# Routed experts fed by slot from DRAM, and a two and four step split of the wide experts

## The reference, cut to what matters

```python
top_val, top_idx = lax.top_k(xf @ router_w, 2)
gates = softmax(top_val)
# for each expert e, on the rows xb of the tokens that chose it:
y = (silu(xb @ w_gate[e]) * (xb @ w_up[e])) @ w_down[e]   # 1024 -> 2816 -> 1024
out[token] += gate * y
```

## Time and profile before

| | us |
|---|---|
| time before, median of 3 runs | 1365.17 (1364.94 to 1366.44) |
| the profiled execution | 1365.75 |
| its span | 1363.9 |
| PE busy | 1295.7 |
| DVE, ACT, POOL busy | 674.4, 555.1, 154.5 |

### The profile page before, as it was taken

The page is one execution under the profiler, slowest core; times in us unless marked ns, Lnnn a source line. Parts: engine busy times, 40 slices in busy tenths (PEclk is TensorE's granted clock), DMA queues, the critical chain, the costliest instruction groups (busy, mean ns, idle before and its releaser), DMA issues.

```text
span 1363.9 us, 25579 instructions
## 1 busy us (share of the span) xinstructions
PE 1295.7 (95%) x10975; PEld 1027.5 (75%) x10975; DVE 674.4 (49%) x894; ACT 555.1 (41%) x843; POOL 154.5 (11%) x201
## 2 busy tenths in 40 slices
PE   7999999999999999999999999799999999979994
PEld 7978988788888987988755777487555577747762
DVE  5766555766666565654510763265101076326512
ACT  5466444533346456644311651254000065225401
POOL 6300000000000800000122011203020201220200
PEclk9999999999999999999999999999999999999998
DMA  9307533455554413652799989998999999999895
GB/s 380 129 1 295 218 136 123 155 185 185 185 202 153 152 35 127 262 198 96 294 418 421 421 343 368 420 420 350 394 421 420 421 420 417 368 420 420 342 412 241
DMA packets 55150, 387.48 MB, mean 284 GB/s; under 512 B 6368, under 2 KB 6752, under 8 KB 9216
## 3 DMA queue, kind: packets, MB, share of 16 engines
q1 hardware_dynamic: 54112, 384.07, 70.8%
q10 hardware_dynamic: 432, 1.08, 0.2%
q0 software_dynamic: 496, 0.74, 0.2%
HBM read 383.77 MB, written 2.10 MB: 283 GB/s over the span
## 4 chain that ended last, share of the span: by engine, by line
PE 82%; DMA 8%; DVE 4%; ACT 3%; issue 1%; SPq 0%; ACTq 0%; DVEq 0%
PE banks L2268 21%; PE banks L1988 14%; PE banks L1989 14%; PE banks L1990 14%; DMA added<-in_pieces_dram 8%; PE banks L2192 6%; PE banks L2194 3%; PE banks L2227 3%; PE banks L2243 2%; PE banks L2139 1%; PE banks L2354 1%; PE banks L2167 1%; PE banks L2002 1%; PE banks L2012 1%; DMA raw<-in_pieces_dram 1%
## 5 line engine op out<-in xcount | busy, mean ns | idle before, releaser
L1455 DVE TENSOR_TENSOR w_low<-raw,w_high 128x2048 fp32r<-128x2048 f32 x93 | 214.5, 2308 | 138.1 <-ACT w_high L992 138.0
L992 ACT ACTIVATE w_high<-raw 128x2048 fp32r<-128x2048 f32 x93 | 178.2, 1918 | 105.4 <-PE banks L2194 65.5
L2268 PE MATMUL banks<-added,token_rows 128*32 128x128 f32 (+2 forms) x3088 | 154.5, 299 | 12.0 <-DMA added<-in_pieces_dram 8.9
L2268 PEld LDWEIGHTS banks<-added,token_rows 128*32 128x32 f32 (+1 forms) x3088 | 116.7, 118 | 49.4 <-issue 18.3
L1988 PE MATMUL banks<-rows,w_high 128*128 128x256 f32 x480 | 136.8, 285 | 3.1 <-DVE rows L1456 2.4
L1989 PE MATMUL banks<-rows,w_high 128*128 128x256 f32 x480 | 135.8, 283 | 0.0
L1990 PE MATMUL banks<-rows,w_low 128*128 128x256 f32 x480 | 135.8, 283 | 0.0
L2192 PE MATMUL banks<-rows,w_high 128*128 128x512 f32 x352 | 124.5, 398 | 1.3 <-DVE rows L1456 1.3
L1455 DVE TENSOR_TENSOR added_low<-added,piece_high 128x1024 fp32r<-128x1024 f32 x80 | 95.7, 1223 | 42.5 <-ACT piece_high L992 25.7
L1450 DVE TENSOR_SCALAR turned<-banks 128x128 f32<-128x128 f32 (+2 forms) x36 | 12.3, 342 | 188.0 <-PE banks L2354 188.0
L2194 PE MATMUL banks<-rows,w_low 128*128 128x256 f32 x352 | 98.8, 281 | 0.0
(11 more groups left out here) (259 smaller groups left out, 2315.5 us busy)
## 6 DMA issues: line engine op xcount, KB each, us to landing
raw<-in_pieces_dram SPq DMA_DIRECT2D x195, 1024.0 KB, 9.2
added<-in_pieces_dram SPq DMA_DIRECT2D x162, 1024.0 KB, 18.3
phase<-in_mem_dram SPq DMA_DIRECT2D x2, 1024.0 KB, 6.5
early<-in_constants_dram SPq DMA_DIRECT2D x1, 1088.0 KB, 13.7
h_res<-in_x_dram SPq DMA_DIRECT2D x2, 512.0 KB, 4.2
phase<-in_mix_norm_post_dram SPq DMA_DIRECT2D x2, 512.0 KB, 4.1
phase<-in_xa_norm_post_dram SPq DMA_DIRECT2D x2, 512.0 KB, 6.3
kept<-h_res SPq DMA_DIRECT2D x2, 512.0 KB, 10.2
```

The lines of the kernel that those rows point to most:

```text
L992: return act.activation(out_, in_, ACT.Copy, scale=scale)
L1455: return dve.tensor_tensor(out_, in_, plain(high), ALU.subtract)
L2268: return pe.matmul(dst, stay, move, start=start, stop=stop, skip_group_check=True)
```

## The change

Rows no longer come from a matmul with `place` (but for the first unit's). In the first layer POOL writes zeros to a new DRAM tensor `by_slot` of 8 x 256 rows. After routing, DVE works out for each token and each of its two choices the row number 256 * expert + rank, and POOL scatters the normed rows there, in four indirect DMAs of 128 rows. For each unit from the second on, POOL loads the first rows of its expert into a new tile `slot_rows` (128 + 32 rows for class 3, 64 for class 1, 32 for class 0), and PE turns them by transposes (`turn_rows`), in three turns for class 3 and in one otherwise. In the first unit these turns stand at its fourth and fifth step. `xn_high` and `xn_low` move into two slots of the ring that are filled later, and the space gives the ring an eleventh new slot, 17 in all. The wide experts are cut into steps (0, 2) and (2, 6) in place of (0, 3) and (3, 6).

```diff
-ADDED = 2 * SPLIT + 4
+ADDED = 2 * SPLIT + 5
-UNITS = ((1, 0, 6), (0, 0, 3), (3, 0, 6), (0, 3, 6), (2, 0, 6), (6, 0, 6), (5, 0, 3), (4, 0, 6), (5, 3, 6), (7, 0, 6))
+UNITS = ((1, 0, 6), (0, 0, 2), (3, 0, 6), (0, 2, 6), (2, 0, 6), (6, 0, 6), (5, 0, 2), (4, 0, 6), (5, 2, 6), (7, 0, 6))
...
-ROWS_AT = {WIDE_STEPS: {(1, "up"): 0, (2, "up"): 1, (3, "up"): 2, (4, "up"): 3, (5, "up"): "spread"},
-           WIDE_STEPS // 2: {(0, "up"): 0, (1, "up"): 1, (1, "out"): 2, (2, "up"): 3, (2, "mid"): "spread"}}
+ROW_TURNS = [ROW_PAIRS if u == 0 else 3 if STRAIGHT[u] == 3 else 1 for u in range(COUNT_UNITS)]
+ROW_LOADS = [0 if u == 0 else 2 if STRAIGHT[u] == 3 else 1 for u in range(COUNT_UNITS)]
+ROWS_AT = {(WIDE_STEPS, 3): {(1, "up"): 0, (2, "up"): 1, (3, "up"): 2, (5, "up"): "spread"},
+           (WIDE_STEPS, 1): {(2, "up"): 0, (5, "up"): "spread"},
+           "first": {(3, "up"): 0, (4, "up"): 1, (4, "out"): 2, (5, "up"): "spread"},
+           (2, 1): {(0, "up"): 0, (1, "mid"): "spread"},
+           (4, 1): {(1, "up"): 0, (3, "mid"): "spread"}}
...
+def row_turn(u, i):
+    if STRAIGHT[u] < 3:
+        return 0, MOST[STRAIGHT[u]], 0, KT
+    return (0, P, i * KT // 2, (i + 1) * KT // 2) if i < 2 else (1, QUARTER, 0, KT)
...
-        xn_low = sb("xn_low", [P, TT, D], F32R)
-        xn_high = sb("xn_high", [P, TT, D], F32R)
+        xn_high, xn_low = (added_low[:, i, :].rearrange("p (t d) -> p t d", t=TT) for i in (2 * SPLIT - 2, 2 * SPLIT - 1))
+        slot_rows = sb("slot_rows", [P, 2, D])
...
-        ring = [RAW + (2 * SPLIT + i) % ADDED for i in range(ADDED)] + [(more_from + i) % RAW for i in range(RAW)]
+        ring = [RAW + i for i in (6, 7, 8, 9, 0, 1, 2, 3, 10, 4, 5)] + [(more_from + i) % RAW for i in range(RAW)]
...
+                if c == more_from + 8:
+                    sp.wait_ge(h_kept, TT * 16)
+                    sp.wait_ge(row_high, TT)
+                if c == more_from + 9:
+                    sp.wait_ge(gathered, ROW_PAIRS)
...
+            chain(pool.memset(zeros[:, :], 0.0))
...
+                if layer == 0:
+                    for b in range(EXPERTS * TT):
+                        pool.dma_start(by_slot[b * P:(b + 1) * P, :], zeros[:, :]).then_inc(zeroed, 16)
...
-            def places(e):
...
+            def load_rows(u):
+                n = UNITS[u][0]
+                for block in range(ROW_LOADS[u]):
+                    count = (MOST[STRAIGHT[u]] if STRAIGHT[u] < 3 else P) if block == 0 else QUARTER
+                    first_row = n * SEQ + block * P
+                    pool.dma_start(slot_rows[0:count, block, :], by_slot[first_row:first_row + count, :]).then_inc(rows_in, 16)
+            pool.wait_ge(zeroed, EXPERTS * TT * 16)
+            pool.wait_ge(row_gained, TT)
+            pool.wait_ge(indexed, 1)
+            for choice in range(2):
                 for t in range(TT):
+                    at = choice * TT + t
+                    pool.indirect_dma_start(by_slot[:, :],
+                                            bass.IndirectOffsetOnAxis(ap=slot_index[:, at:at + 1].bitcast(U32), axis=0),
+                                            xn[:, t, :], None).then_inc(scattered, 16)
+            pool.wait_ge(scattered, 2 * TT * 16)
+            pool.wait_ge(row_high, TT)
+            pool.wait_ge(row_low, ROW_PAIRS)
+            load_rows(1)
             pool.wait_ge(rank_ready, 2)
-            for e in range(COUNT_UNITS):
-                if e + 1 < COUNT_UNITS:
-                    places(e + 1)
-                places_of_rows(e)
+            places_of_rows(0)
+            for u in range(1, COUNT_UNITS):
+                pool.wait_ge(spread_full, u)
+                if u + 1 < COUNT_UNITS:
+                    load_rows(u + 1)
+                places_of_rows(u)
...
+            def turn_rows(u, i, bank):
+                block, count, k0, k1 = row_turn(u, i)
+                pe.wait_ge(rows_in, 16 * LOADS_TO[u])
+                for k in range(k0, k1):
+                    ins = pe.transpose(banks[:, bank, (k - k0) * count:(k - k0 + 1) * count],
+                                       slot_rows[0:count, block, k * P:(k + 1) * P], ident[0:count, 0:count])
+                ins.then_inc(gathered, 1)
```

More of the change, by code:

```diff
@@ L193, in is_last @@
     return s == UNITS[u][2] - 1
-ROWS_AT = {WIDE_STEPS: {(1, "up"): 0, (2, "up"): 1, (3, "up"): 2, (4, "up"): 3, (5, "up"): "spread"},
-           WIDE_STEPS // 2: {(0, "up"): 0, (1, "up"): 1, (1, "out"): 2, (2, "up"): 3, (2, "mid"): "spread"}}
+assert set(STRAIGHT.values()) <= {0, 1, 3}
+ROW_TURNS = [ROW_PAIRS if u == 0 else 3 if STRAIGHT[u] == 3 else 1 for u in range(COUNT_UNITS)]
+TURNS_BEFORE = [sum(ROW_TURNS[:u]) for u in range(COUNT_UNITS + 1)]
+ROW_LOADS = [0 if u == 0 else 2 if STRAIGHT[u] == 3 else 1 for u in range(COUNT_UNITS)]
+LOADS_TO = [sum(ROW_LOADS[:u + 1]) for u in range(COUNT_UNITS)]
+assert UNITS[0][1:] == (0, WIDE_STEPS) and ROW_TURNS[1] == 3
+ROWS_AT = {(WIDE_STEPS, 3): {(1, "up"): 0, (2, "up"): 1, (3, "up"): 2, (5, "up"): "spread"},
[3 more added lines that the diff above has]
+           (4, 1): {(1, "up"): 0, (3, "mid"): "spread"}}
 def rows_at(u, s, where):
     _, start, stop = UNITS[u]
-    what = ROWS_AT[stop - start].get((s - start, where))
-    return None if u + 1 == COUNT_UNITS and what != "spread" else what
+    if u + 1 == COUNT_UNITS:
+        return "spread" if ROWS_AT[stop - start, 1].get((s - start, where)) == "spread" else None
+    return ROWS_AT[(stop - start, ROW_TURNS[u + 1]) if u else "first"].get((s - start, where))
+def row_turn(u, i):
+    if STRAIGHT[u] < 3:
+        return 0, MOST[STRAIGHT[u]], 0, KT
+    return (0, P, i * KT // 2, (i + 1) * KT // 2) if i < 2 else (1, QUARTER, 0, KT)
 def lay_out(given):
@@ L508, in build @@
         gathered, x_ready = sem("gathered"), sem("x_ready")
+        zeroed, indexed, scattered, rows_in = sem("zeroed"), sem("indexed"), sem("scattered"), sem("rows_in")
+        more_in = [sem(f"more_in{u}") for u in range(COUNT_UNITS)]
+        more_turned, more_ready = sem("more_turned"), sem("more_ready")
         spread_full, spread_ready = sem("spread_full"), sem("spread_ready")
@@ L1864, in route @@
                     take_rows(pair)
+                for t in range(TT):
+                    ins = dve.scalar_tensor_tensor(out=slot_at[:, t, :], in0=iota[:, 0:EXPERTS], scalar=float(SEQ),
+                                                   in1=rank[:, t, :], op0=ALU.mult, op1=ALU.add)
+                chain(ins)
+                for n, which in enumerate((first, second)):
+                    ins = dve.tensor_tensor(slot_if_chosen[:, n, :, :], which, slot_at, ALU.mult)
+                chain(ins)
+                chain(dve.tensor_reduce(slot_number, slot_if_chosen.rearrange("p n t e -> p (n t) e"), AX_X, ALU.add))
+                dve.tensor_copy(slot_index, slot_number).then_inc(indexed, 1)
                 counted = logits[:, 0, :]
@@ L2451, in wait_rows_taken @@
                     elif what is not None:
-                        pe.wait_ge(x_ready, ROW_PAIRS * (e + 1) + what + 1)
+                        pe.wait_ge(x_ready, TURNS_BEFORE[e + 1] + what + 1)
                 def next_rows(s, where):
@@ L2462, in next_rows @@
                     else:
-                        gather(e + 1, what, bank)
+                        turn_rows(e + 1, what, bank)
                 def serial_expert():
@@ L2529, in expert @@
                 if e:
-                    pe.wait_ge(x_ready, ROW_PAIRS * (e + 1))
+                    pe.wait_ge(x_ready, TURNS_BEFORE[e + 1])
+                    turn_more_rows(e, groups)
                 if groups == 3:
@@ L2657, in _ @@
                     pe.wait_ge(row_low, pair + 1)
-                    gather(0, pair, pair)
+                    gather(pair, pair)
                 experts(pe, "pe", expert)
```

64 lines of the change are left out of this document (51 added, 13 removed).

## The result

The changed kernel takes 1374.1 us (median of 3 runs, 1372.22 to 1376.06), before 1365.17. The ratio is 1.0059, with a 95% interval of 1.004 to 1.0077: slower by 8.1 us, between 5.5 and 10.5. The forecast was 1366.6, in a range of 1356 to 1377. So the time lies in the range, but the likeliest case, no change, did not come; the sum is 7.5 us short. The profiled execution's span is 1372.3 us, 8.4 more than before.

What follows compares the result with a forecast made beforehand. The prediction took the experts as bound by DMA, the weight stream full at about 421 GB/s except in four dips. Standstill -12.0 and traffic +13.4 gave +1.4 us, 1367.2 profiled, 1366.6 as median, range 1356 to 1377.

Steps and rivals of the forecast that it cites:

- The standstill, 30.4 to 18.4: Weight stream's dips at the ends of units 1, 3, 6 and 8: two vanish, 9.5 and 8.9 us remain, -12.0 us.
- The traffic, 13.4 us: Scatter and row loads beside the weight stream: 5.64 MB cost their bytes at 421 GB/s, +13.4 us.
- small transfers cost more than their bytes: Rival, above all at the scatter: half as much again gives 1373.3 us, the row's 40 us gives 1393; chance 0.13.
- the balance: Main case, whole kernel: standstill -12.0 and traffic +13.4 give 1366.6 us, own range 1362 to 1371; chance 0.45.
- The cut: Wide experts: units 1 and 6 lose a step, units 3 and 8 gain one, each adding 7.6 us of standstill.
- The slot, 2.5 us per remaining dip: Weight ring: the seventeenth slot takes one more piece before the ring fills, 2.5 us less in every remaining dip.
- Zeros, DVE, POOL: 0: First layer's zeros, DVE's small instructions and POOL's issues fall in idle time: 0; uncovered zeros would cost 20 us.
- The first unit's rows, 0 to 3 us, taken 0: PE's wait in unit 0 for rows scattered and loaded, ready at 696.5 to 736.4, needed at 719.3: taken as 0.
- PE starts the long units slowly, 1371.6: Rival at units 3 and 8: 5 us more low clock in both, PE loses 2.5 us each, 1371.6; chance 0.17.
- Traffic hidden: Rival, stream between the dips: half the added traffic costs nothing, 1359.9 us, or all, 1353.2; chance 0.17.
- no dip in the long units: Rival at units 3 and 8: the long unit doesn't fill the ring, 18.4 us go, 1348.2 us; chance 0.08.
- not doing what it says: Rival: unit counts above their class run `turn_more_rows`, 1 MiB and 16 transposes more; no chance worth a number.

Runs made afterwards that it cites:

- second trace of before: The kernel before, nothing changed, profiled once more: 1362.64 us in one run, with 26.0 us of dips in place of 30.4.
- experiment 9: On experiment 1, loads of 32 or 64 rows land on every fourth or second partition, so some rows differ from the reference's: 1356.4 us, ratio 0.9943.
- experiment 11: Changed kernel, two-and-four cut kept, loads of 32 or 64 rows on every fourth or second partition, so some rows differ: 1371.23 us, ratio 1.0037.
- experiment 3: Changed kernel without the scatter, a semaphore increment in place of each indirect transfer: 1370.83 us, ratio 1.0032.
- experiment 1: Changed kernel with the wide experts cut into three and three steps again, nothing else: 1362.61 us, ratio 0.9972.
- experiment 7: On experiment 1, the eleventh new slot of the ring left unused, 16 slots in place of 17: 1366.64 us, ratio 1.0014.
- experiment 8: As experiment 7, with scatter and loads of slot rows left out too, so only turns and zeros remain: 1352.95 us, ratio 0.9906.
- experiment 4: Changed kernel without the zeros and without the loads of slot rows: 1363.25 us, ratio 0.9978, beside 0.9981 with the zeros.
- experiment 2: Changed kernel without the loads of slot rows, a semaphore increment in place of each of the 13: 1363.52 us, ratio 0.9981.

## Why the prediction was right and where it was wrong

*The standstill, 30.4 to 18.4.* Right in its mechanism: 17.8. That the change of -12.6 meets the -12.0 so closely is in part luck, since against the second trace of before it is -8.2. The dips of units 1 and 6 went away, and those of units 3 and 8 came to 9.8 and 8.0 (forecast 9.5 and 8.9). The step of class 3 measured 22.6 us, as worked out. A turn of eight takes 0.61 us where 0.8 was taken.

*The traffic, 13.4 us.* This is the step that failed, by its size: "most of a landing time of a lone transfer is latency ... so I take the volume". The bytes are as counted, and nothing of them was hidden (share 1.01). But loads into 32 or 64 neighbouring partitions slowed the weight stream beside them, and the term is 13.4 + 5.8 = 19.2. Experiments 9 and 11 change the partitions alone: the first takes 4.0 us off the time, the second 4.7 us off the excess. It lies within the bounds given, 0 to 40, but I chose the volume between them, and the rows of before could not speak against it: its loads in the expert part are all 128 partitions wide.

The prediction left out a rule that bears on this. The Trainium skill (SBUF — State Buffer, Door 1: The DMA port swizzle) has the DMA side of SBUF as 16 ports, and partitions 0 to 31, and 0 to 63 as well, reach only 8 of them. If loads of 32 and 64 rows move at half rate and hold the stream up as long, they cost their bytes' time once more, an estimate of 7 x 0.31 + 2 x 0.62 = 3.4 us; the windows show 4.7 that go with the stride. By the page's formula a stride of two or four reaches all 16. The Trainium skill (SBUF — State Buffer, Can I just issue two DMAs to hit both halves?) calls one transfer spanning all 128 partitions the only way there; the loads of experiment 9 filled 32 or 64 of them, and the stream beside them kept 423 GB/s. The runs show that it is the partitions; that the ports are the reason is argued, no run here looks at them.

*The rival "small transfers cost more than their bytes", 1373.3.* Nearest to the time, and half right: its price came, its place ("the scatter above all") did not. The scatter costs 3.7 us for 5.0 us of bytes (experiment 3). That the time lies inside the range is owed to this rival, which stretched the range upwards; the balance's own range ended at 1371.

*The cut.* The prediction added its parts up and never asked what the cut alone was worth. Its own terms would have said it: the steps added to units 3 and 8 cost 2 x 7.6 = 15.2 us of standstill, and with turns, slot and traffic in place units 1 and 6 have next to no dip left for the shorter units to save. Experiments 1, 7 and 8 give the ledger by ratios: turns -12.8, traffic +14.8, slot -5.7, cut +11.9, each uncertain by some 2.5 to 4 us. Each step starts where the one before ends, so that their sum, +8.2, is the measured ratio and proves nothing; and each price holds for this order.

*The slot, 2.5 us per remaining dip.* Right: 5.4 to 5.7 for two.

*Zeros, DVE, POOL: 0.* Right for the zeros (experiment 4); no wait on DVE's or POOL's new work appears in the chain.

*The first unit's rows, 0 to 3 us, taken 0.* Right. The scatter began at 687.60 (685.5 forecast), POOL waited 16.48 us for it, and the loads went out at 708.95; the rows were there at 721.35 with no wait. It was close: the estimate of 3.2 us per landing didn't come, the medians are 13.5 us for the scatter and 9.1 for loads of 512 KB beside the full stream, and the last packet of the rows started 1.2 us before the turn.

*PE starts the long units slowly, 1371.6.* Not the cause in the trace of the changed kernel. Windows where units 3 and 8 start:

```profile
872.00:884.00 12.00, 11.45 (x100) 9.03 (x93) 6.86 (x9) 5.01 (x6) 0.00 (x0) 0.84 1.02 421
...
1222.00:1240.00 18.00, 18.00 (x221) 14.69 (x213) 11.47 (x14) 9.54 (x11) 0.00 (x0) 1.00 1.02 421
```

Unit 3 had 12 x 0.16 / 0.5 = 3.8 us at half clock, where the earlier trace rows had 3.6, and unit 8 had none, where the earlier trace rows had 6.8. The 128-row matmuls of unit 3 start at 875.96, when the clock is back at full. Experiments 2 and 11 show losses of some 3 us by it and the two traces of before differ by it: the mechanism exists, and its size differs from one execution to the next.

*Traffic hidden; no dip in the long units; not doing what it says.* All out: the rate beside the loads fell, the dips are 9.8 and 8.0 us, and L2311 ran at the class expected.

*The 2.3 us before the experts.* No step spoke of them, and 1.1 of them is seen as chance between executions. They are part of the 8.4 us of the one profile, and a reason to take the change's price from the ratio.

*The chances.* They don't add up as stated. The parts give slower 0.05 + 0.25 = 0.30, faster 0.04 + 0.14 + 0.08 = 0.26 and same 0.44, where the prediction has 0.34, 0.27 and 0.39. Slower, which came, had less than a third by its own parts.

## What to carry to other kernels

When a change bundles several edits around one shared resource, price each alone against the state that the others leave: here the turns and the slot had already emptied the dips that the new cut was to save. A full DMA share is not a full rate: read GB/s beside it, and ask of every small load that runs beside a stream which partitions it fills. Thirty-two rows on every fourth partition cost their bytes; thirty-two neighbouring rows cost that and some half a microsecond of everyone else's. Before a term of a few us is called right by one trace, take a second one: here two traces of one kernel differ by 4.4 us of standstill.

## What the runs showed of the hardware that was not expected

- A load of 64 rows into neighbouring partitions brought a stream of 420 GB/s to 341 to 347 over 6 us at an unchanged share of 1.02; with the same rows on every second partition it stayed at 419 to 423. A load of 128 rows, twice the bytes, left it at 420.
- An indirect scatter of 4 x 128 rows of 4 KB beside a full stream cost 3.7 us, its bytes' 5.0 us within the interval, and the weight packets beside it took 309 ns, 313 without it.
- Two executions of the same program (the kernel before) reached the same instruction 1.1 us apart, at 678.74 and 679.85 us, and their streams stood still for 30.4 and 26.0 us. In one, units 3 and 8 began their 128-row matmuls at half clock for 1.1 and 1.9 us; in the other at full clock.
- Landings beside the full stream took 13.5 us (scatter) and 9.1 us (plain load), medians for 512 KB each; POOL's own load of 512 KB before the experts took 3.9 us.
